# Odd layer of a two-layer DiT forward pass: router logits from raw rows, experts' rows stored normalised, scale and shift applied where a block's rows are turned

## The reference, cut to what matters

```
x  = x + mx[2] * y_x                                   # mixer's output, gated
hx = rmsnorm(x, norm_ffn[l]) * (1.0 + mx[4]) + mx[3]   # mx[3], mx[4]: one value per feature
g_logit = hx @ wg + bg ;  e_logit = hx @ we + be       # 4 groups, 8 experts in each
g_sel   = argmax(g_logit) ; top 2 experts of that group, softmax weights
y       = sum over 32 experts e of c_e * ((silu(hx @ w1_e) * (hx @ w3_e)) @ w2_e)
x  = x + mx[5] * y ;  return rmsnorm(x, norm_final)
```

## Time and profile before

| | |
|---|---|
| median of 3 runs | 1005.98 us (1004.57 to 1009.06) |
| profiled execution | 1004.57 us, its span 1002.8 us |
| PE / DVE / ACT / POOL busy | 94% / 40% / 25% / 21% |
| HBM read, written | 315.00 MB, 22.31 MB |
| mean over the span | 336 GB/s |

### The profile page before, as it was taken

How to read it: one execution, slowest core, us unless ns; L and a number is a source line. 1 busy time by engine, 2 the same in 40 slices (tenths; PEclk the granted TensorE clock), 3 DMA queues, 4 the chain that set the end, 5 groups by cost and what they waited for, 6 DMA issues and landing times.

```text
span 1002.8 us, 17308 instructions
## 1 busy us (share of the span) xinstructions
PE 939.3 (94%) x5907; PEld 595.9 (59%) x5908; DVE 404.2 (40%) x887; ACT 246.9 (25%) x538; POOL 215.4 (21%) x309
## 2 busy tenths in 40 slices
PE   5999998999997999998989899999988999999886
PEld 3444447657885555555555475877875555555553
DVE  4149496477637111101001489565344212222124
ACT  4120002365233222211212240132133111111112
POOL 1007501110002333331431000000003333333220
PEclk9999999999998999999999999999999999999999
DMA  9985454799446999999999899893557999999996
GB/s 347 340 247 205 143 167 157 263 330 373 167 150 228 337 407 405 405 406 407 407 406 407 323 383 390 264 327 115 195 173 264 398 400 407 406 406 402 404 406 233
DMA packets 129948, 315.86 MB, mean 315 GB/s; under 512 B 28988, under 2 KB 60756, under 8 KB 129861
## 3 DMA queue, kind: packets, MB, share of 16 engines
q1 hardware_dynamic: 114152, 295.93, 79.5%
q0 software_dynamic: 10800, 12.72, 3.8%
q10 hardware_dynamic: 4908, 6.03, 1.7%
HBM read 315.00 MB, written 22.31 MB: 336 GB/s over the span
## 4 chain that ended last, share of the span: by engine, by line
PE 70%; DMA 11%; DVE 8%; SPq 4%; issue 3%; ACT 2%; POOLq 0%; DVEq 0%; POOL 0%; ACTq 0%
PE ps L1217 19%; PE ps L1017 14%; DMA ring<-in_moe_w 9%; PE ps L1243 8%; PE ps L1069 8%; PE ps L1027 4%; DVE RAB L2504 4%; SPq L748 3%; PE ps L1185 3%; PE ps L960 3%; PE ps L1227 2%; PE ps L1394 1%; DMA mod_rows<-in_norm_ffn 1%; PE ps L1475 1%; PE ps L1491 1%
## 5 line engine op out<-in xcount | busy, mean ns | idle before, releaser
L1217 PE MATMUL ps<-ring,RT 128*64 128x256 f32 x2096 | 254.5, 392 | 18.9 <-DMA ring<-in_moe_w 15.4
L1217 PEld LDWEIGHTS ps<-ring,RT 128*64 128x64 f32 x2096 | 160.0, 140 | 86.2 <-issue 14.5
L1017 PE MATMUL ps<-RT,ring 128*128 128x512 f32 (+1 forms) x544 | 182.1, 493 | 1.1 <-DVE RT L2462 1.1
L1017 PEld LDWEIGHTS ps<-RT,ring 128*128 128x128 f32 x544 | 102.2, 190 | 77.3 <-issue 70.6
L2339 DVE TENSOR_TENSOR RT<-RT,ps 64x256 f32<-64x256 f32 x64 | 27.1, 423 | 260.0 <-ACT RT L1817 159.2
L1243 PE MATMUL ps<-ring,RT 128*64 128x512 f32 x424 | 100.4, 593 | 2.1 <-DVE RT L2345 1.8
L1817 ACT ACTIVATE RT<-ps 64x256 f32<-64x256 f32 x64 | 24.1, 377 | 247.6 <-PE ps L1217 219.7
L2504 DVE SCALAR_TENSOR_TENSOR RAB<-RM,chan,RAB 128x512 f32<-128x512 f32 x120 | 79.7, 742 | 0.0
L2767 POOL DMA_INDIRECT pair_out<-RH,sidx_all x62 | 62.8, 1013 | 55.4 <-POOL sidx_all L2764 50.0
L2743 POOL DMA_INDIRECT RH<-hrow,idx x7 | 7.7, 1106 | 292.5 <-DMA hrow<-RH 291.0
L2755 POOL DMA_INDIRECT RH<-hrow,sidx_all x56 | 59.2, 1057 | 49.4 <-issue 29.0
(11 more groups left out here) (314 smaller groups left out, 1036.2 us busy)
## 6 DMA issues: line engine op xcount, KB each, us to landing
ring<-in_moe_w SPq DMA_DIRECT2D x354, 512.0 KB
ring<-in_w_mod SPq DMA_DIRECT2D x96, 512.0 KB
ring<-in_odd_w_in SPq DMA_DIRECT2D x24, 512.0 KB
ring<-in_even_w_in SPq DMA_DIRECT2D x20, 512.0 KB
ring<-in_even_w_out SPq DMA_DIRECT2D x8, 512.0 KB
RAB<-in_moe_w SPq DMA_DIRECT2D x8, 512.0 KB, 8.0
RAB<-pair_out SPq DMA_DIRECT2D x8, 512.0 KB, 8.7
ring<-in_odd_w_out SPq DMA_DIRECT2D x8, 512.0 KB
```

What stands on the lines that cost most here:

```text
L1017: mm = pe.matmul(bank, w[:, c, P * ft:P * (ft + 1)], moving[:, c, :], start=(c == 0), stop=(c == NCH - 1))
L1217: mm = pe.matmul(bank[CAP * k:CAP * (k + 1), 0:BLK], xt(c), rows_at(w[k], c), start=(c == 0), stop=(c == NCH - 1))
```

## The change

All of it is in the odd layer; layer 0 keeps its code.

- `columns_of(1, 3)` and `columns_of(1, 4)` give the columns in another order, features p*4+j, and do so with 8 matmuls of 64 columns each where there were 2 of 128. The router's weights are loaded in that feature order.
- While DVE waits for the mixer it multiplies `WR` by the scale (`scaled_router`) and by the shift and sums over a partition's chunks (`shift_sums`).
- PE does the four half tiles of the output projection in a row, one small matmul for the shift's part of the logits, and turns `X` itself, not the normalised rows. ACT (three banks) and DVE (one) copy it to `hT` unchanged.
- The row factor 1/rms is applied to the logits (36 values for each token) in `scalar_tensor_tensor`. DVE still writes tile 1's normalised rows to `H`; ACT writes tile 0's. `H` is stored as it stands. `tile_rows` is gone, and so are the warming matmuls ahead of `lgT`.
- Groups and experts are chosen for both tiles in one pass.
- `first_turned` stands behind the first of the four blocks of `slot_rows(1, 1)`, ahead of it before.
- Scale and shift are applied by ACT where a block's turned rows are copied to `XT`: eight instructions of 64 columns where there was one of 512. PE's first `U` waits for these one by one.

```diff
@@ PE
+                if (l, v // 3) == (1, 1):
+                    for j in range(4):
+                        for hf in (0, 1):
+                            out = bank[64 * hf:64 * hf + 64, 0:16].rearrange("p (a j s) -> p a j s", a=2, j=4)[:, :, j, :]
+                            mm = pe.matmul(out, modrow[:, v, j:BLK:4], pick[:, hf::2, :], start=True, stop=True)
...
+            def raw_turned(t, a):
+                pe.wait_ge(x_updated, xu_mix[1] - 2 * tiles_of[1] + 2 * NORM_ORDER[3].index(t) + a + 1)
+                bank = open_bank("rT", t, a)
+                for j in range(4):
+                    mm = pe.transpose(bank[:, P * j:P * (j + 1)], X[:, t, 512 * a + j:512 * (a + 1):4], ident)
...
+            def raw_logits():
+                shift_logits()
+                raw_turned(1, 0)
+                raw_turned(1, 1)
+                raw_turned(0, 0)
+                raw_tile_logits(1)
+                raw_turned(0, 1)
+                token_logits(1, 1)
+                raw_tile_logits(0)
+                token_logits(1, 0)
...
-            for h in (0, 1):
-                mixed_half(1, h)
-            norm_and_logits(1, (), lambda h: mixed_half(0, h))
+            for t in (1, 0):
+                for h in (0, 1):
+                    mixed_half(t, h)
+            raw_logits()
...
-            first_turned(1)
-            slot_rows(1, 1)
+            slot_rows(1, 1, behind_first=lambda: first_turned(1))
@@ ACT
+            def raw_logits():
+                squares_of(1, 0, 0)
+                for t, a in ((1, 0), (1, 1), (0, 0)):
+                    raw_turned(t, a)
+                rows_stored(1)
+                feature_logits(1, 1)
+                squares_of(1, 0, 1)
+                feature_logits(1, 0)
+                act.wait_ge(row_factor, 1)
+                act.activation(H[:, 0, :], X[:, 0, :], ACT.Copy, scale=rstd[:, 3, 0:1]).then_inc(x_normed, 1)
+                rows_stored(0)
...
+                def modulated_rows(out, bank, first=False):
+                    bank = bank.rearrange("p (j a s) -> p j a s", j=4, a=2)
+                    for c in range(NCH):
+                        a, j = c // 4, c % 4
+                        ins = act.activation(out[:, j, a, :], bank[:, j, a, :], ACT.Identity,
+                                             scale=row_cols[:, 1, a, j, LATENT:LATENT + 1], bias=row_cols[:, 0, a, j, LATENT:LATENT + 1])
+                        if first and c < NCH - 1:
+                            ins.then_inc(first_modulated, 1)
@@ DVE
+            def scaled_router_of():
+                dve.tensor_tensor(scaled_router, WR[:, :, :], by_chunk[1].broadcast_to([P, NCH, 64]), ALU.mult).then_inc(router_scaled, 1)
+                step(dve.tensor_tensor(shifted_router, WR[:, :, 0:n], by_chunk[0].broadcast_to([P, NCH, n]), ALU.mult))
+                dve.tensor_reduce(shift_sums, shifted_router.rearrange("p c n -> p n c"), AX.X, ALU.add).then_inc(router_shifted, 1)
...
+                done(dve.scalar_tensor_tensor(out=logits[:, 0, :], in0=bank[:, 0:n], scalar=rstd[:, 3, 0:1],
+                                              in1=shift_of_logits, op0=ALU.mult, op1=ALU.add))
+                both = slice(0, 2)
+                group_choice(1, both)
+                two_choices(both)
```

More of the change, by code:

```diff
@@ L156, in norm_and_logits @@
         by_rows(l, *((1, 0) if early else (0,)))
+    def raw_logits():
+        mixed(1, 0)
+        add(("shift logits",), "dve")
+        add(("rT", 1, 0), "act")
+        add(("rT", 1, 1), "act")
+        add(("rT", 0, 0), "act")
+        add(("lgT", 1, 1), "act")
+        add(("rT", 0, 1), "dve")
+        add(("lg", 1, 1), "dve")
+        add(("lgT", 1, 0), "act")
+        add(("lg", 1, 0), "dve")
     transposed(0, *NORM_ORDER[0])
@@ L1054, in token_logits, with shift_logits, raw_tile_logits @@
                 close(mm)
+            def shift_logits():
+                bank = open_bank("shift logits")
+                pe.wait_ge(router_shifted, 1)
+                close(pe.matmul(bank[:, 0:GROUPS + EXPERTS], ones, shift_sums, start=True, stop=True))
+            def raw_turned(t, a):
[3 more added lines that the diff above has]
+                    mm = pe.transpose(bank[:, P * j:P * (j + 1)], X[:, t, 512 * a + j:512 * (a + 1):4], ident)
+                    freed(mm)
+                close(mm)
+            def raw_tile_logits(t):
+                for a in (0, 1):
+                    drained(pe, "rT", t, a)
+                pe.wait_ge(router_scaled, 1)
+                bank = open_bank("lgT", 1, t)
+                for c in range(NCH):
+                    p = 64 * (c % 2)
+                    mm = pe.matmul(bank[p:p + 64, 0:P], scaled_router[:, c, :], hT[:, c, P * t:P * (t + 1)],
+                                   start=(c < 2), stop=(c >= NCH - 2))
+                    freed(mm)
+                close(mm)
+            def raw_logits():
[8 more added lines that the diff above has]
+                token_logits(1, 0)
             def tile_rows(l, t):
@@ L1138, in slot_rows @@
                         mm.then_inc(slot_used, 1)
+                    if b == 0 and behind_first is not None:
+                        behind_first()
                 close(mm)
@@ L1203, in U @@
                     n, b = i * PER_LOOP + (n0 + q), q % 2
-                    pe.wait_ge(xT_ready, n + 1)
+                    by_chunk = l == 1 and isinstance(i, int) and (i, q) == (0, 0)
+                    if not by_chunk:
+                        pe.wait_ge(xT_ready, n + 1)
                     if not start:
@@ L1215, in up @@
                     for c in range(NCH):
+                        x = xt(c)
                         for k in (0, 1):
-                            mm = pe.matmul(bank[CAP * k:CAP * (k + 1), 0:BLK], xt(c),
+                            mm = pe.matmul(bank[CAP * k:CAP * (k + 1), 0:BLK], x,
                                            rows_at(w[k], c), start=(c == 0), stop=(c == NCH - 1))
@@ L1838, in more @@
                             act.wait_ge(x_xT_full, x)
-                            act.activation(XTX.rearrange("p j a s -> p (j a s)"), bank, ACT.Copy).then_inc(x_xT_ready, 1)
+                            if l == 1:
+                                modulated_rows(XTX, bank).then_inc(x_xT_ready, 1)
+                            else:
+                                act.activation(XTX.rearrange("p j a s -> p (j a s)"), bank, ACT.Copy).then_inc(x_xT_ready, 1)
                             act.wait_ge(x_up_full, x)
@@ L2059, in _ @@
                 squares_of(1, 1, h)
-            norm_and_logits(1, ())
+            raw_logits()
             router_exps(1)
```

80 lines of the change are left out of this document (64 added, 16 removed).

## The result

The changed kernel takes 1010.06 us in the median of 15 executions (1003.66 to 1014.4), before 1006.24 in the same comparison (1002.93 to 1013.91, 15). The ratio is 1.0032, 95% interval [1.0016, 1.0048]: slower by 3.2 us. Timed again later (`e16_after_again`) beside 35 executions of before, it gave 1.0021 [1.0005, 1.0038], 2.1 us. The prediction was 1004.7 (1001.0 to 1008.5), 1.3 us faster. The profiled execution took 1010.06, its span 1008.3, 5.5 over that of before.

A forecast was written before the change was run, and what follows sets the result against it. The odd layer's experts were taken as bound by the DMA weight stream, its end moving one to one with `routed`. Columns +1.4 and `routed` -2.7 gave -1.3 us: median 1004.7 us, range 1001.0 to 1008.5.

The forecast's parts named there:

- Step 7: Copies of turned rows: ACT's eight pieces cost PE 3.0 us against 6.6 us to spare; no effect on the end.
- the first of the signs: Sign of a wrong prediction: the DMA share has holes in the experts' stretch.
- The rival that the clock falls: PE pauses about 2 us ahead of the ranks and its clock drops: +2.7 us, 1008.7; chance 0.08.
- Step 1: Two vectors turned to columns in PE's chain, 32 matmul passes in place of 8: +1.4 us.
- Steps 2 to 4: Mixer's tail ends earlier, tile 0's logits -3.3 us, choosing for both tiles together +0.6: `one_hot` moves -2.7.
- Step 5: Slots: a block fills PE's wait ahead of `first_turned`; first expert's matmuls move another -0.45 us, `routed` unaffected.
- Step 6: POOL's gathers start earlier after stores and indices; `routed`, following them, moves -2.5 to -3.3 us, taken as -2.7.
- the -2.7 of the sum: Forecast move of `routed` in us, taken from the choice and added to the columns' +1.4.

The follow-up runs named there:

- e16_after_again: The changed kernel once more, with no edit, timed beside 35 executions of before; median 1007.48 us, ratio to before 1.0021.
- e18_regular_plain: Changed kernel with plain copies, leaving out scale and shift, for all blocks but the first and the extra one; ratio to before 1.0042.
- e17_extra_plain: Changed kernel with the extra block's turned rows copied plainly in one instruction, without scale and shift; ratio to before 1.0011.
- e12_columns_twice: `e8_no_gather_wait` with each vector's 8 column matmuls (16 passes) issued twice; 1009.5 us, ratio to before 1.0029.
- e2_bank: Changed kernel with the second slots bank placed in bank 5 in place of bank 2; ratio to before 1.0019.
- e3: Changed kernel with PE taking the second block piece by piece and DVE scaling and shifting the extra block in two instructions; ratio to before 1.0021.
- e9: `e8_no_gather_wait` plus filler matmuls on constants in the extra block's two waits, in layer 0's extra blocks too; ratio to before 1.0031.
- e10: Changed kernel with slots in bank 5, columns apart, twelve warming matmuls, no second-gather wait, plain copies for all blocks but the first; ratio to before 1.0013.
- e1: Changed kernel with one plain copy, without scale and shift, for every block but the first; ratio to before 1.0009.
- e15: Changed kernel with eight warming matmuls ahead of the ranks in place of four; ratio to before 1.0021.
- e11: Kernel before without SP's wait for the second gather; ratio to before 0.9992.
- e8_no_gather_wait: Changed kernel: slots in bank 5, columns apart, twelve warming matmuls, second block piecewise, extra block scaled by DVE, no second-gather wait; ratio to before 1.0001.
- e13_best: All edits of `e8_no_gather_wait`, with eight warming matmuls ahead of the ranks in place of twelve; 1007.6 us, ratio to before 1.0011.
- e4_columns: Kernel before with five more matmuls of 64 columns, results unused, behind each of the two vectors turned to columns; ratio to before 1.0043.

## Why the prediction was wrong

**Step 7 failed**: "the one extra block pays +1.8 us. Together 3.0 us of PE against 6.6 us that PE has to spare: no effect on the end". Two things were wrong in it. The cover was read from a sum over the whole stretch, 6.6 us in seven waits. They stand at 925 to 981 us, and a late PE at 833 us can't use them: there it is the loads that wait for slots. And the price was more than the copy: eight pieces, 2.47 us (0.31 each; I took 0.30), make PE wait 2.56 us, 1.9 more than before (forecast: 1.8), and in five of six profiles the clock was at half behind this wait, which added 1.7 to 2.9 us to `U` (5.36 to 6.55 in place of 3.67). So in those five the block costs 3.6 us or more, slots come back late, and 30 to 60 us further on the DMA engines lack work worth some 3 us. The second block cost more than forecast too, 1.5 to 1.7 us in place of 1.2, but `e18_regular_plain`, where it costs nothing, has the same third part. The holes in the DMA share are the first of the signs that the prediction named for being wrong. `e18_regular_plain` shows the gap with this block alone, `e17_extra_plain` shows it gone with this block alone taken out. The rival that the clock falls was priced at +2.7 with a chance of 0.08 and put at the ranks; it happened near there in some profiles, but above all behind a wait that I had costed at 1.8 us.

**Step 1** (columns +1.4) was right: 2.09 us, which moved the start of the next matmuls by 1.2. I had reasoned from the loads' mean. The Trainium skill (TensorE: Matmul & The Clock Gate, LDWEIGHTS) takes a load's time in ns as its columns divided by 1.2, by an estimate 53 ns for 64 of them and 1.7 us for the 32 passes. The trace has 0.065 us each at this place, between the page's and my 0.073, and `e12_columns_twice` 0.060 for each pass added.

**Steps 2 to 4** (`one_hot` -2.7) were right: the ranks start 95.32 us behind the columns where they stood at 96.56, -1.24; with the columns' +1.2 taken off this is -2.5. PE ran through the half tiles, and both tiles' choice took 3.4 us from 756.03 to the operation that releases the ranks.

**Step 5** held for the first expert only after the bank was changed. The new plan puts `slots 1` into the bank of the first `U`, which then waits 1.13 us for DVE's last read. I hadn't looked at which banks the new uses fall into; `e2_bank` took that wait away.

**Step 6** had the right size for the wrong reason. `routed` does not follow the end of POOL's gathers. DVE's wait of 1.93 us, which ends with the third gather, stands in 6 of 20 profiles (before, e3, e9, e10, e12, e17) and lasts 1.9 to 2.0 us in each; in the others DVE writes beside the gathers. Both sorts occur with the same routing code, and with the same distance of DVE's operation from the second gather, so what decides is open. In the profile after it is absent, the stores land 1.6 us earlier, with the columns' 1.2 taken off, rather than 2.6, and SP's gate is the second gather's landing. The result, -2.5 without the columns, is close to the -2.7 of the sum only because these cancel. Over six profiles of the changed code without DVE's wait and without a slower clock ahead of the ranks (after, e1, e2, e15, e16, e18) the second part has a mean of 105.2, against 106.96 and 106.31 (before, e11). With the two that have the wait or a slower clock (e3 108.4, e17 106.4) the mean of the eight is 105.7.

**What stays open.** By the parts, the change is worth -1.4 at the start of the stream (-0.9 with all eight profiles) and +2.6 behind it: +1.2 to +1.7 us. Measured were +3.2 (interval 1.6 to 4.8) and +2.1 (0.5 to 3.8), so the parts fit the second and hardly the first. In the two comparisons the changed kernel's mean granted clock was 0.9829 and 0.9859, and that of before, on record for the later comparisons only, 0.9861 to 0.9875; time and mean clock go together (correlation -0.93 over the changed kernel's 15 executions), so the rest is likely spells that single profiles catch or miss. That was only argued: the profiles are one execution each. No version with the change came out faster than before: the best, `e8_no_gather_wait`, is level with it. Why `e13_best`, which starts the stream 3.3 us earlier than before, gains nothing of it is not settled either; its own profile has a spell in the second block and small gaps at 784 and 790.

## What to carry to other kernels

Spare time of an engine is local. Before costing work at nothing because the engine waits somewhere for its data, ask how far ahead of the stream it is at that very place and where its next waits stand; one irregular step (an extra block, the first block) pays in full what all regular ones hide. A wait that stands in one profile may be absent from most others: read a second profile, or a neighbour kernel's, before a forecast follows from it. And compare kernels by distances between fixed points of the program, with windows behind the place in question, when single executions scatter by more than the effect.

## What was not expected of the hardware

- The granted clock falls in spells worth 1.7 us of TensorE each; the end of layer 0, whose code is the same, lies up to 6.6 us apart between profiles, with more spells in the late ones.
- A PE that the profile shows as busy can lose its clock: 3.1 us into 3.6 us of matmuls with a moving side of 2 and 8 it fell to 0.50 for 7 us (`e4_columns`), while 2.09 us of those with 4 were followed by a spell in one profile only (`e3_pieces`) of those that have them.
- More warming isn't monotone: at 762 to 780 us a spell stands in 5 of 7 profiles of the changed code with four warming matmuls, in 3 of 3 with eight and in none of 6 with twelve, the last of which held up the ranks by 1.5 us. The six differ from most others in bank and columns too, so this is a count and not a shown cause.
